# A fused attention and Fourier layer: the second half of w_o is loaded ahead of the first group's inputs, and VectorE's work on w_o is put in another order

## The reference, cut to what matters

```python
def gated_merge(p, attn_out, w_f, w_o):
    ga = p[..., GA0:F0]
    fu = p[..., F0:GF0]
    gf = p[..., GF0:D_IN]
    y = jnp.concatenate([attn_out * jax.nn.silu(ga), fourier_mix(fu, w_f) * jax.nn.silu(gf)], axis=-1)
    return y @ w_o
...
        x_new = x + gate[:, None] * gated_merge(p, attn, w_f[l], w_o[l])
...
    return rmsnorm(x, final_g)
```

## Time and profile before

| | |
|---|---|
| median of 3 runs | 1484.06 us (1478.99 to 1485.08) |
| time of the profiled execution | 1484.06 us |
| its span, first to last instruction | 1482.2 us |
| mean granted clock of TensorE | 0.979 |
| PE busy | 1423.0 us (96%) |
| DVE busy | 792.5 us (53%) |
| ACT busy | 599.5 us (40%) |
| POOL busy | 709.5 us (48%) |

### The profile page before, as it was taken

How to read it: one execution, slowest core, us unless ns; L and a number is a source line. 1 busy time by engine, 2 the same in 40 slices (tenths; PEclk the granted TensorE clock), 3 DMA queues, 4 the chain that set the end, 5 groups by cost and what they waited for, 6 DMA issues and landing times.

```text
span 1482.2 us, 22292 instructions
## 1 busy us (share of the span) xinstructions
PE 1423.0 (96%) x7846; PEld 975.3 (66%) x7846; DVE 792.5 (53%) x1235; ACT 599.5 (40%) x806; POOL 709.5 (48%) x366
## 2 busy tenths in 40 slices
PE   6898986999999999999999999999999999999997
PEld 4677873555555555555555555588888788878886
DVE  2667665665565566665565555641230632465452
ACT  3454421445455455455455455622313133431120
POOL 0324221999999999999999999400000000000000
PEclk9998995999999999999999999999999999999999
DMA  9655427000000000000000000392241052477742
GB/s 367 213 145 189 122 52 216 19 12 22 21 11 21 21 11 22 23 11 21 21 11 21 21 11 21 88 252 99 85 149 43 15 219 79 117 215 210 197 145 82
DMA packets 79364, 134.36 MB, mean 91 GB/s; under 512 B 6077, under 2 KB 53445, under 8 KB 78410
## 3 DMA queue, kind: packets, MB, share of 16 engines
q1 hardware_dynamic: 71914, 120.82, 25.7%
q0 software_dynamic: 6672, 12.58, 3.0%
q10 hardware_dynamic: 720, 0.15, 0.0%
HBM read 103.97 MB, written 29.56 MB: 90 GB/s over the span
## 4 chain that ended last, share of the span: by engine, by line
PE 80%; issue 1%; DMA 1%; DVE 1%; ACT 1%; SPq 0%; POOLq 0%; POOL 0%; ACTq 0%; DVEq 0%
PE pv_ps L1181 17%; PE max_ps L1151 11%; PE s_ps L1167 10%; PE s_ps L1168 9%; PE acc L63 7%; PE acc L65 7%; PE acc L64 7%; PE o_ps L63 4%; PE o_ps L65 4%; PE o_ps L64 3%; PE row_ps L1189 1%; DMA gin<-rest_scratch 1%; DVE chunk_max L1062 0%; DMA blk_q_hilo<-q_scratch 0%; ACT prob L1006 0%
## 5 line engine op out<-in xcount | busy, mean ns | idle before, releaser
L967 POOL TENSOR_TENSOR prob_sum<-prob_sum,prob 128x1024 f32<-128x1024 f32 x217 | 520.8, 2400 | 33.4 <-ACT prob L1006 17.3
L1062 DVE TENSOR_REDUCE chunk_max<-max_ps 128x1 f32<-128x512 f32 (+1 forms) x640 | 392.9, 635 | 257.8 <-PE max_ps L1151 254.6
L1006 ACT ACTIVATE prob<-s_ps 128x1024 f32<-128x1024 f32 x288 | 295.1, 1025 | 300.1 <-PE s_ps L1168 294.6
L1181 PE MATMUL pv_ps<-prob,v 128*32 128x512 f32 x2304 | 266.9, 596 | 0.0
L1151 PE MATMUL max_ps<-k_hi,blk_q_hilo 128*128 128x512 f32 (+1 forms) x640 | 247.2, 404 | 13.2 <-DMA blk_q_hilo<-q_scratch 10.6
L1167 PE MATMUL s_ps<-blk_q_hilo,k_hi 128*128 128x512 f32 x576 | 233.8, 406 | 1.7 <-DVE blk_q_negm L1075 0.9
L1168 PE MATMUL s_ps<-blk_q_negm,k_lo 68*128 68x512 f32 x576 | 229.4, 398 | 0.0
L1151 PEld LDWEIGHTS max_ps<-k_hi,blk_q_hilo 128*128 128x128 f32 x640 | 120.4, 192 | 102.9 <-issue 38.3
L1181 PEld LDWEIGHTS pv_ps<-prob,v 128*32 128x32 f32 x2304 | 65.1, 109 | 137.9 <-issue 134.1
L63 PE MATMUL acc<-hh,w_rest_hi 128*128 128x512 f32 x384 | 151.1, 393 | 0.2 <-ACTq L1490 0.2
L64 PE MATMUL acc<-hl,w_rest_hi 128*128 128x512 f32 x384 | 150.4, 392 | 0.0
(11 more groups left out here) (266 smaller groups left out, 1867.4 us busy)
## 6 DMA issues: line engine op xcount, KB each, us to landing
xt_raw<-in_xt SPq DMA_DIRECT2D x16, 512.0 KB, 5.5
x_tok<-in_x SPq DMA_DIRECT2D x16, 512.0 KB, 4.8
blk_q_hilo<-q_scratch SPq DMA_DIRECT2D x32, 256.0 KB, 2.6
h_raw<-in_xg SPq DMA_DIRECT2D x4, 2048.0 KB, 9.8
rest_scratch<-stage SPq DMA_DIRECT2D x32, 256.0 KB, 2.2
gin<-rest_scratch SPq DMA_DIRECT2D x16, 512.0 KB, 10.6
x_res<-in_x SPq DMA_DIRECT2D x16, 512.0 KB, 3.7
out_x<-res SPq DMA_DIRECT2D x16, 512.0 KB, 3.0
```

Of the source, the lines that this page charges most:

```text
L967: nc.gpsimd.tensor_tensor(acc_pool[slot][:], acc_pool[slot][:], probs(slot, j)[:], ALU.add).then_inc(s_psum, 1)
L1006: nc.scalar.activation(probs(slot, j)[:], s_ps[slot2(slot, j)][:], ACT.Exp).then_inc(s_exp, 1)
L1062: nc.vector.reduce_max(chunk_max[:, qt, kc:kc + 1], max_ps[u % 2][:, 0:MAX_CHUNKS[kc]], X_AXIS).then_inc(s_mfree, 1)
L1181: last = nc.tensor.matmul(pv_ps[row:row + QUAD], k.v[:, 2 * j + e, kvh, half * QUAD:(half + 1) * QUAD], probs(slot, j)[:, e * QB:(e + 1) * ...
```

## The change

On SP, the second half of w_o is issued ahead of the six loads of group 0, and no longer behind them. On DVE, after gates 0 to 3, att_gate(0) comes first, then gates 4 to 7, then the eight w_o_low in order, with y_lo of the attention half after w_o_low(4). The number of instructions and of bytes is the same.

```diff
             sp.wait_ge(s_z, Z_TILES)
+            sp.dma_start(w_o_raw[1][:], w_o_v[1]).then_inc(s_w[1], 16)
             load_group(0)
-            sp.dma_start(w_o_raw[1][:], w_o_v[1]).then_inc(s_w[1], 16)
             sp.wait_ge(s_dft, RADIX * GROUPS)
...
-            for c in range(4):
+            att_gate(0).then_inc(s_gated, 1)
+            for c in range(4, KD):
+                gate_w_o(c)
+            for c in range(KD):
                 w_o_low(c)
-            att_gate(0).then_inc(s_gated, 1)
-            gate_w_o(4)
-            dve.wait_ge(s_yhi, 1)
-            nc.vector.tensor_tensor(y_lo[0][:, ATT, :], yin[0][:, ATT, :], y_hi[0][:, ATT, :].bitcast(F32),
-                                    ALU.subtract).then_inc(s_ylo, 1)
-            for c in range(5, KD):
-                gate_w_o(c)
-                w_o_low(c - 1)
-            w_o_low(KD - 1)
+                if c == 4:
+                    dve.wait_ge(s_yhi, 1)
+                    nc.vector.tensor_tensor(y_lo[0][:, ATT, :], yin[0][:, ATT, :], y_hi[0][:, ATT, :].bitcast(F32),
+                                            ALU.subtract).then_inc(s_ylo, 1)
             dve.wait_ge(s_y, RADIX * GROUPS)
```

## The result

The changed kernel takes 1491.67 us (median of 5 runs, 1488.01 to 1492.33) against 1484.06 (5 runs). The ratio is 1.0057, with a 95% interval of 1.003 to 1.0084, so it is slower: the medians differ by 7.6 us and the ratio stands for 8.5, where +10.0 was forecast. The profiled execution has a span of 1490.5 us, 8.3 more than before.

The account below looks back on a forecast made before the run. PE, busy nearly the whole span, was taken as the bound. Stand 9.1, less 1.1 given back at group 1, plus 2.0 for the clock gave +10.0 us: 1494.1 us, 0.67% slower, range 1488 to 1498.5.

Parts of the forecast that it names:

- PE sets the end, and nothing behind the hand-over gives back: From output group 1 on PE is busy 155.39 of 156 us; moving that group's start moves the end equally.
- The row from landing to product: On DVE, att_gate, four gates, five w_o_low and y_lo put PE's first output product 14.0 us after gin lands.
- Where gin lands: On SyncE's queue, w_o ahead of group 0's loads moves gin's landing from 1285.7 to 1290.5, 4.8 us later.
- the bounds of 0.4 and 8.8: gin's delay: 0.4 us for one issue if transfers run side by side; w_o's 8.8 us if loads begin after it.
- The one by bytes: Estimate of gin's delay: 2.10 MB of w_o at 400 GB/s, 5.2 us, plus 0.4 for issue, landing at 1291.3.
- The estimate from 1 MB of x_res: Group 1's loads lost 1.9 us behind 1 MB, so 2 MB of w_o cost 3.8; gin lands at 1289.5.
- The split between the edits: Of 9.1 us of PE stand before the output products, 4.3 from the reordering alone, 4.8 from the later landing.
- The 1.1 us at group 1: PE's stands of 1.1 us, put on DVE's lateness for group 1, vanish since its inputs are ready in time.
- The clock: After the 9 us stand PE's clock falls to 0.50 for 4.5 us of work, costing 2.0 us (1.5 to 2.8).
- nothing hid the transfer: Claim that loads move beside w_o, gin landing at 1286.1: only +5.1 to +5.6 us, 1489.2 to 1489.7; chance 0.18.
- there was no gain: Claim that early w_o readies DVE sooner and PE never stands at the hand-over: 1.1 us gained, 1483.0; chance 0.01.
- Rival 2: Group 0's loads begin only when w_o has landed: gin at 1294.5, +14.8 us, 1498.9; chance 0.12.

Follow-up runs that it names:

- both shortened rows: Changed kernel with w_o_low 0 to 3 back ahead of att_gate(0), or with y_lo after w_o_low(0): ratio intervals against the kernel before end at 1.0027 and 1.0030.
- the added matmuls: Changed kernel plus 30 filler matmuls of 512 columns on PE ahead of the first output product: ratio 1.0051.
- y_lo after w_o_low(0): Changed kernel with the attention half's y_lo after w_o_low(0) in place of w_o_low(4): ratio interval ends at 1.0030.
- swap, x_res last: Kernel before with the queue swap alone, plus group 1's loads issued ahead of x_res: ratio interval 0.9972 to 1.0001.

## Why the prediction was right, and where not

*PE sets the end, and nothing behind the hand-over gives back.* Right: 163.0 or 163.1 us in every profile.

*The row from landing to product.* Right, 14.0 predicted and 13.98 measured, and 9.4 and 9.44 with four steps fewer. It is the step that carries the slowdown, and both shortened rows moved PE as it says. It holds where w_o has landed ahead of gin.

*Where gin lands.* 4.8 us later were taken, 3.9 came, inside the bounds of 0.4 and 8.8. It is the larger part of what the sum has too much. The stand came out at 8.2 in place of 9.1. By the packets both estimates missed what happens. The one by bytes took 5.2 us for w_o and 0.4 for the issue, and the loads' first packet was in fact 5.3 us later. But it let the loads take as long behind w_o as before, and they were 1.4 us shorter. The likely reason, not tested, is that before they were issued one by one, 0.65 us apart, while the engines were partly idle (share 0.81), and now all stood in the queue when w_o was through (share 1.02). The estimate from 1 MB of x_res gave 3.8, near the 3.9; that it doubled a row of another transfer makes the closeness partly luck. In the nine profiles with w_o issued first, gin lands 5.2 to 6.2 us ahead of the last Fourier matmul, and in the three with the loads first 8.8 to 9.5, so the delay is 3.4 us in the mean.

The Trainium skill ("DMA: Bandwidth & Descriptors", section "Bandwidth") lists its 341 GB/s for 1 MB for transfers issued from GpSimd; w_o is issued by SyncE. At that figure w_o takes 6.2 us, an estimate, and its packets do start over 6.2 us, slow at first (1273.88 to 1280.06). As the price that gin pays, it would have put gin still later than 1290.5, and there the trace does not bear it out.

*The split between the edits.* Wrong. The prediction gave 4.3 us of the stand to the reordering alone and 4.8 to the later landing. The queue swap alone costs 0.5 us in its profile and at most 0.05%, 0.7 us, by its interval; the reordering alone costs 10.9. The step that failed is the sentence that took gin's old landing plus 14.0 for the half change: that row of 14.0 holds four gates on w_o, which without the swap lands last. The total was not harmed, since with both edits gin does land after w_o, but whoever had undone the swap on the strength of that split would, by the profiles, have lost 2 to 3 us more.

*The 1.1 us at group 1.* Right for the changed kernel: gap 0.39, nothing left. It is part of the sum because the stand in front gave the loads time. The prediction put all of it on group 1's inputs; 0.31 of it was the Fourier half of group 0's y_lo, at product 49.

*The clock.* 2.0 us taken, 1.7 in the profile of the changed kernel, 1.4 in its second one, and 1.7 to 2.0 by the added matmuls. The loss measured is 0.45 of the low time, 1.7 of 3.8 us (0.43 us between starts against 0.235). The Trainium skill ("TensorE: Matmul & The Clock Gate", section "Terms") has it at half; the trace agrees nearly, with 0.45. The premise that the stand of 1.70 us in the Fourier part brings the clock down is only true of some executions. That stand is in all twelve profiles, and the clock fell behind it in four of them (before, changed, the first of "y_lo after w_o_low(0)", and "swap, x_res last"). In the changed kernel's second profile it did not. These are its row in the timeline of PE and the stretch around it, with the granted clock third from the end:

```profile
1253.64 0.47 PE L63 MATMUL acc<-tab,zo_hi 128*128 128x512 f32 x1 [1.70 <-issue]
...
1253.00:1262.00 9.00, 8.36 (x49) 7.31 (x50) 0.99 (x2) 4.91 (x6) 0.00 (x0) 1.00 0.01 2
```

After the long stands of 7.55 to 9.06 us the clock was low in all three profiles that have one with no matmuls put in (changed, changed once more, new order only).

In all, from the last Fourier matmul: 8.2 - 1.0 + 1.7 = +8.9, and that matmul itself was 0.6 us earlier in this profile, for reasons that lie before the change: +8.3 in the span. The rivals' times did not come: nothing hid the transfer, and there was no gain. Rival 2 was right that the loads move only when w_o is nearly through, but put gin at 1294.5, against 1289.6 on the time line of before, since it added the full 8.8 and 12.3 us. The absolute time hangs on the level of the set of runs: in a later set the changed kernel took 1487.78 us against 1480.63, below the 1488 at which the predicted range began, and still 7.2 us slower.

## What to carry to other kernels

On an engine that works in order, put work whose inputs are there ahead of a wait for a transfer, and put what the critical engine wants first straight behind it; count the steps between the landing and the instruction that the critical engine waits for, since each is paid in full. Where two edits meet in such a row, price each alone with all its waits before splitting the effect: here one costs nothing, the other at least as much as both.

## What the runs showed of the hardware that I had not expected

A stand's length alone does not decide the clock. 2.95 us left it at 1.00, 3.10 in the same kernel brought it to 0.50 about 1 us after work had resumed, and 3.07 in another before it resumed. The price was 0, 1.5 and 2.6 us. The stand of 1.70 us in the Fourier part was followed by a low clock in four of twelve profiles.

The six loads hardly overlap with the 2 MB ahead of them in the queue. In the nine profiles with w_o first, their first packet starts 0.5 us or less before w_o's last one, and 5.2 to 5.4 us later than in the three with the loads first. gin lands only 2.6 to 4.3 us later, since from their first packet to att_gate the loads take 8.8 to 9.7 us behind w_o and 10.7 to 11.4 without it.

The last Fourier matmul starts anywhere from 1289.1 to 1295.1 us in kernels whose PE work is alike up to it. Most of that spread is there early: the 1500th of PE's matmuls starts between 305.4 and 310.3 us. The four profiles with the low clock in the Fourier part add 1.6 us to it. What makes the early part differ was not looked into.
